# Eight instead of four of the 22 weight steps of each FFN output product computed block-wise with seven products, in a new order

## Chip, cores and metric

One NeuronCore of a Trainium2 chip runs the whole program. The metric is the device time of one execution in microseconds (us), median of several runs. The program has one launch and computes one forward pass of a small two-layer transformer for 256 tokens.

## What is computed

The reference, cut to what matters here. `x` is 256 x 2048, D_MODEL = 2048, D_FF = 5632.

```python
for layer in range(2):
    if layer == 0:   # MLA attention plus attention to 256 memory tokens
        mix = mla_mixer(rms_norm(x, ...), positions, mem, ...)
    else:            # differential attention; keys and values from shared_kv(x)
        k1, k2, v = shared_kv(x, positions, shared_kv_norm, shared_w_kv)
        mix = diff_mixer(rms_norm(x, ...), positions, mem, k1, k2, v, ...)
    x = x + rms_norm(mix, attn_norm_post)
    u = rms_norm(x, ffn_norm_pre[layer]) @ ffn_w_in[layer]        # 2048 -> 11264
    c = conv_b + causal convolution of width 3 of u over the tokens
    h = gelu(c[:, :5632]) * c[:, 5632:]
    x = x + rms_norm(h @ ffn_w_out[layer], ffn_norm_post[layer])  # 5632 -> 2048
```

Everything is float32. The change concerns `h @ ffn_w_out[layer]` in both layers: (256 x 5632) times (5632 x 2048).

## The kernel before

**Arithmetic.** A float32 product is made from three fast ones: every weight block and every activation is split into a high part (the value rounded to the fast format, written by ScalarE) and a low part (value minus high part, written by VectorE); TensorE adds high x high, high x low and low x high into one PSUM bank.

**Steps and rings.** Weights come in steps of 128 partitions x 1024 columns (512 KB: two 128-row chunks of 512 output columns). SyncE (SP) loads a step into `w_raw`, a ring of R = 4 slots; ScalarE (ACT) writes `w_hi`, VectorE (DVE) writes `w_lo`, TensorE (PE) uses both. The semaphores `hi_ready`, `lo_ready` and `step_used` count steps. ACT and DVE are written out by hand in one fixed order: `splits_to(s)` issues all splits up to step s, and epilogues stand between such calls. So a wait inside an epilogue holds back the splits behind it.

**FFN input product (IN0, IN1).** `ffn_in` and `merged_product` (L765 to L806) run 11 iterations of 16 steps per layer: 8 steps for four gate chunks, 8 for four value chunks. In even steps the w_hi products come first, in odd steps the w_lo products. The loops on ACT (L2240 to L2256) and DVE (L3115 to L3140) split weights and, between the splits, form h: `correction` and `corrected` (L3058, L3060), `first_tap`, `other_taps` (L3072), `gate`, `gate_times_value` (L3082), `hi_half`, `lo_half` (L3088). Each loop is in two parts, `(0, PAIRS // 2)` and `(PAIRS // 2, FJ)`. In the first part four more DVE operations on blocks of h (`odd_forms`, `even_forms`), one ACT copy (`sums_hi`, L2236) and one DVE subtraction (`forms_lo`, L3112) make the sums of blocks that the output product needs. The ACT loop stands behind a wait for `x_spilled`: the sums lie where x was, so x has gone to DRAM before.

**Handing over to layer 0's FFN.** After its last operation on the norm (`rstd_row`, L1783), ACT goes into the loop. DVE first waits for that row, adds the late part of the memory values to `vm_b` (L3148, two operations), and goes into its loop.

**FFN output product (OUT0, OUT1).** The output columns are four tiles of 512; each has 22 steps of 2 x 128 rows of the weight. A half is two tiles. For most steps (`plain`, L1277) PE does 2 chunks x 2 token blocks x 3 terms = 12 matmuls of 128x128 by 128x512. For `PAIRS` = 4 of the 22, the same step of both tiles is taken together as a `unit`: as a 2 x 2 block product (two token blocks, two chunks, two tiles) with seven block products instead of eight, 21 matmuls instead of 24. A unit has four entries in the ring, `left` (6 matmuls), `corner` (3), `odd` (6), `even` (6), but two raw slots only. DVE makes the sums of weight blocks (`out_split`, L2392, L2401, L2404); the raws are released by the last of them (`unit_sums`). The order of entries is `out_order`; their slots are `out_slots`. In the first half the order is 9 plain steps of the tile, then units 0 to 3 with 2 plain steps after each, then the rest of that tile, then 18 plain steps of the other tile; the second half is the same. From `UNIT_STARTS` on, for `WIDE` = 40 entries, a fifth slot is used; there the slot's last user is five entries back, at the first unit's `even` entry and elsewhere four.

**Folds and epilogues.** Products shared by several outputs are put together when a half's last unit is done (`fold_copies` on ACT, `fold` on DVE: five operations of 512 columns, L2857 to L2861, and one of 1024, L2865, after the first tile's last step). PE starts the second tile of the half when `folded` says so. `wide_epilogue` then squares the tile on ACT (L2062) and multiplies it by the gain on DVE (L2884). The last tile of a product is `held`: its last HOLD = 4 steps are done for token block 0 first, then for block 1, and its first block needs all four of them. `splits_to(s0 + ends[3])`, which splits the last step, stands behind the third tile's L2884.

**Pool.** GpSimd's queue sends x to DRAM ahead of the FFN (L672), loads the gain row at the start of the output product (L667), and brings x back after the last unit of the second half (L677).

Of the kernel before, what the change touches and what calls it, by code (L numbers as in the profile page):

```python
# [22 lines left out]
P = 128  # L23
# [9 lines left out]
M = 256  # L33
# [24 lines left out]
PAIRS = 4  # L58
# [4 lines left out]

def out_order():
# [13 lines left out]
    ends, unit_ends, unit_starts = [], [], []  # L80
    for half in range(2):
        ks = list(range(PAIRS, FSTEPS))
        for k in ks[:CUT]:
            plain(2 * half, k)
        rest = ks[CUT:]
        unit_starts.append(len(entries))
        for p in range(PAIRS):
            unit(half, p)
            if p == PAIRS - 1:
                unit_ends.append(len(entries))  # L90
            n = 2 if p < PAIRS - 1 else len(rest)
            for k in rest[:n]:
                plain(2 * half, k)
            rest = rest[n:]
        ends.append(len(entries))
        for k in ks:
            plain(2 * half + 1, k)
        ends.append(len(entries))
# [6 lines left out]
WIDE = 40  # L105


def out_slots():
# [11 lines left out]
    assert all(slots[e] == e % R for e in list(range(CUT)) + list(range(OSTEPS - R + 1, OSTEPS)))  # L120
# [124 lines left out]
def program(nc, x_in, mem_in, positions, inv_freq, w, vec, out):  # L245

    with ExitStack() as ctx:
# [19 lines left out]
        raw_flat = w_raw[:, :, :].rearrange("p r n -> p (r n)")  # L267
# [3 lines left out]
        sx_hi = at("sx_hi", [P, PAIRS // 2, 1024], F32R, X0)  # L271
        sx_lo = at("sx_lo", [P, PAIRS // 2, 1024], F32R, X0 + 8 * KB)
# [114 lines left out]
        def unit_quarters(r):  # L387


            a = 1024 * (r % R)  # L390
            assert r % R < R - 1
            return raw_flat[:, a:a + 2048].rearrange("p (q n) -> p q n", q=4)
# [108 lines left out]
        x_back = sem("x_back")  # L501
        ostd_ready = sem("ostd_ready")
# [131 lines left out]
        def _(pool):  # L634
# [56 lines left out]
        def _(pe):  # L691
# [362 lines left out]
            def scores_b(t):  # L1054

                if t in (1, 3, 4, 8, 9):
                    pe.wait_ge(e_ready, T0_B + (t - 1 if t >= 8 else t))
# [211 lines left out]
            def out_product(s0, t0, layer, h_done, turn_done=None):  # L1269
# [22 lines left out]
                def unit(e, kind, p):  # L1292
# [7 lines left out]
                    def s(form, cols, bank):  # L1300
                        o = 256 * form + P * (p % 2)
                        return terms(bank, sx_hi[:, p // 2, o:o + P], sx_lo[:, p // 2, o:o + P],
# [5 lines left out]
                    if kind == "corner":  # L1308
                        return s(3, a, 0)
                    if kind == "odd":  # L1310
                        s(0, a, 1)
                        return s(1, b, 6)
                    s(2, a, 5)
                    return h(1, 1, b, 3)

                for half in range(2):
# [3 lines left out]
                    for e in range(first, OUT_ENDS[2 * half]):  # L1320
                        kind, j, k, _ = OUT_ENTRIES[e]
# [9 lines left out]
                        if half == 0 and k == FSTEPS - 2:  # L1331
                            pe.wait_ge(h_lo, h_done)
                        mm = plain(e, k, 2, range(TT)) if kind == "plain" else unit(e, kind, k)
# [337 lines left out]
        def _(act):  # L1671
# [369 lines left out]
            def fold_copies(s0, half):  # L2041
# [3 lines left out]
                nc.scalar.activation(fold_now[:, 0], ps[:, 1, :], ACT.Copy)  # L2045
# [153 lines left out]
            def ffn_epilogues(layer, s_in, t_in, g_count):  # L2199
# [33 lines left out]
                def sums_hi(i):  # L2233

                    act.wait_ge(s_sums, val(layer * (PAIRS // 2) + 1, 1, i))
                    nc.scalar.activation(sx_hi[:, bass.ds(i, 1), :].rearrange("p a n -> p (a n)"),  # L2236
                                         scratch[:, 0].rearrange("p a b -> p (a b)"), ACT.Copy)\
                        .then_inc(s_hi, 1)

                act.wait_ge(x_spilled, 16 * (layer + 1))  # L2240
                for first, end in ((0, PAIRS // 2), (PAIRS // 2, FJ)):
                    with act.Fori(first, end) as i:
                        for j in range(2):
                            for k in range(DSTEPS):
# [10 lines left out]
                                if ahead == 9 and j == 1 and first == 0:  # L2255
# [102 lines left out]
        def _(dve):  # L2358
# [11 lines left out]
            def out_split(s):  # L2370
# [6 lines left out]
                if kind == "corner":  # L2377
                    nc.vector.tensor_tensor(lo[:, 0:512], unit_quarters(r)[:, 3],
# [8 lines left out]
                if kind == "left":  # L2387

                    quarters, no = unit_quarters(r), raw_no(s0) + r + 1
# [3 lines left out]
                        out_slot(e + 2)[2].rearrange("p (a n) -> p a n", a=2), quarters[:, 0:4:3, :],  # L2393
                        quarters[:, 2].unsqueeze(1).to_broadcast([P, 2, 512]), ALU.add)\
                        .then_inc(odd_sums, 1)
                if kind == "corner":

                    quarters, odd, even = unit_quarters(r), out_slot(e + 1)[2], out_slot(e + 2)[2]
                    dve.wait_ge(step_used, s0 + OUT_USERS[e + 2] + 1)
                    dve.wait_ge(odd_sums, unit_no)  # L2400
                    nc.vector.tensor_tensor(even[:, 0:512], odd[:, 0:512], quarters[:, 3], ALU.add)\  # L2401
                        .then_inc(even_sum, 1)
                    dve.wait_ge(even_sum, unit_no)
                    nc.vector.tensor_tensor(even[:, 512:1024], even[:, 0:512], quarters[:, 1],  # L2404
# [445 lines left out]
            def fold(s0, folds, half):  # L2850
# [199 lines left out]
            def ffn_epilogues(layer, s_in, t_in, g_count):  # L3050
# [28 lines left out]
                def gate_times_value(i):  # L3079
                    dve.wait_ge(pair_dve, val(t_in + 2, 2, i))  # L3080
                    dve.wait_ge(gate_ready, val(g_count + 1, 1, i))
                    nc.vector.tensor_tensor(scratch[:, 1], scratch[:, 0], scratch[:, 1], ALU.mult)\  # L3082
# [224 lines left out]
```

## Time and profile before

| | us |
|---|---|
| median of 3 runs | 2175.74 (2175.74 to 2178.74) |
| the profiled execution | 2175.84 |
| its span | 2174.0 |
| PE busy | 2160.2 (99%) |
| PE weight loads busy | 1870.5 (86%) |
| DVE busy | 1542.9 (71%) |
| ACT busy | 1209.2 (56%) |
| GpSimd busy | 8.9 (0%) |
| DMA | 414.60 MB, mean 191 GB/s |

The 1.84 us between span and time lie outside of what the profile shows. TensorE's granted clock is 9 tenths or more in all of the 40 slices, so no stage is slowed by it. Busy time is the union of an engine's instructions; a matmul's own duration (0.389 us) overlaps with its neighbours', so what a matmul costs is the distance between starts.

### The profile page before, as it was taken

To read this page: it belongs to the slowest core of one execution; us is meant where nothing else is said; L and a number is where in the kernel's file an instruction comes from. 1 tells how busy PE (TensorE), PEld (TensorE's weight loads), DVE (VectorE), ACT (ScalarE), POOL (GpSimd) and SP (SyncE) were. 2 spreads that over 40 slices of the span, in tenths; PEclk is the share of its full clock that TensorE was granted. 3 is DMA by queue.
4 is the path that set the end of the run, shared out by engine and by line. 5 is a ranking of instruction groups with operands and counts; after the bars stand their busy time and mean duration, and the time that the engine had idled before them with its cause. 6 is when DMAs were issued, how large, how long until landed. Compare 5 with 4: busy or idle time off the path is not lost.

```text
span 2174.0 us, 32418 instructions
## 1 busy us (share of the span) xinstructions
PE 2160.2 (99%) x11637; PEld 1870.5 (86%) x11637; DVE 1542.9 (71%) x2172; ACT 1209.2 (56%) x1716; POOL 8.9 (0%) x24
## 2 busy tenths in 40 slices
PE   9999999999999999999999999999999999999998
PEld 8989988888888888888888889888888888888887
DVE  5767756777776767857589877567777776778484
ACT  5745745655555555545465567466555555555353
POOL 0000000000000000000000000000000000000000
PEclk9999999999999999999999999999999999999999
DMA  8565266566566566656756643665655666566665
GB/s 288 176 188 184 82 209 207 175 193 199 178 184 193 186 199 193 213 194 186 249 164 205 196 152 127 202 198 181 204 182 185 191 188 188 183 204 214 200 217 172
DMA packets 202089, 414.60 MB, mean 191 GB/s; under 512 B 12989, under 2 KB 13367, under 8 KB 200719
## 3 DMA queue, kind: packets, MB, share of 16 engines
q1 hardware_dynamic: 200687, 400.29, 58.5%
q0 software_dynamic: 1312, 13.11, 1.7%
q8 instruction: 56, 0.92, 0.2%
q14 instruction: 34, 0.28, 0.0%
HBM read 407.06 MB, written 6.29 MB: 190 GB/s over the span
## 4 chain that ended last, share of the span: by engine, by line
PE 95%; DVE 3%; ACT 1%; issue 1%; DMA 0%; DVEq 0%; ACTq 0%
PE ps L785 27%; PE ps L1277 21%; PE ps L739 20%; PE ps L793 14%; PE ps L823 4%; PE ps L833 3%; PE ps L1518 1%; PE ps L914 1%; DVE scratch L3072 0%; PE ps L1421 0%; PE ps L1044 0%; PE ps L886 0%; PE ps L979 0%; DVE w_lo L2456 0%; ACT w_hi L1738 0%
## 5 line engine op out<-in xcount | busy, mean ns | idle before, releaser
L2456 DVE TENSOR_TENSOR w_lo<-w_raw,w_hi 128x1024 fp32r<-128x1024 f32 x450 | 541.6, 1222 | 261.2 <-ACT w_hi L1738 257.5
L785 PE MATMUL ps<-xT,w_hi 128*128 128x512 f32 x2752 | 657.6, 391 | 0.0
L1738 ACT ACTIVATE w_hi<-w_raw 128x1024 fp32r<-128x1024 f32 (+1 forms) x466 | 475.8, 1042 | 232.6 <-PE ps L739 83.5
L785 PEld LDWEIGHTS ps<-xT,w_hi 128*128 128x128 f32 x2752 | 505.4, 188 | 98.3 <-issue 0.4
L793 PEld LDWEIGHTS ps<-xT,w_lo 128*128 128x128 f32 x2752 | 353.2, 191 | 15.1 <-DVE w_lo L2456 1.6
L793 PE MATMUL ps<-xT,w_lo 128*128 128x256 f32 x2752 | 358.7, 283 | 0.8 <-DVE w_lo L2456 0.8
L2382 DVE TENSOR_TENSOR w_lo<-w_raw,w_hi 128x1024 fp32r<-128x1024 f32 x142 | 171.5, 1223 | 107.4 <-ACT w_hi L1692 106.3
L1277 PE MATMUL ps<-w_hi,hT_hi 128*128 128x512 f32 x624 | 242.8, 389 | 0.0
L1277 PE MATMUL ps<-w_hi,hT_lo 128*128 128x512 f32 x624 | 242.8, 389 | 0.0
L1277 PE MATMUL ps<-w_lo,hT_hi 128*128 128x512 f32 x624 | 242.7, 389 | 0.0
L1692 ACT ACTIVATE w_hi<-w_raw 128x1024 fp32r<-128x1024 f32 x142 | 148.8, 1058 | 133.4 <-PE ps L1277 84.2
L739 PE MATMUL ps<-w_hi,xT 128*128 128x512 f32 x640 | 203.3, 392 | 0.0
L1734 ACT ACTIVATE w_hi<-w_raw,gcol 128x512 fp32r<-128x512 f32 x160 | 106.6, 718 | 62.3 <-PE ps L739 53.0
L739 PEld LDWEIGHTS ps<-w_hi,xT 128*128 128x128 f32 x640 | 120.2, 188 | 24.4
L1277 PEld LDWEIGHTS ps<-w_hi,hT_hi 128*128 128x128 f32 x624 | 117.1, 188 | 24.4
L1277 PEld LDWEIGHTS ps<-w_hi,hT_lo 128*128 128x128 f32 x624 | 117.1, 188 | 24.3
L1277 PEld LDWEIGHTS ps<-w_lo,hT_hi 128*128 128x128 f32 x624 | 117.1, 188 | 24.2
L2443 DVE SCALAR_TENSOR_TENSOR w_lo<-w_raw,gcol,w_hi 128x512 fp32r<-128x512 f32 x160 | 111.9, 748 | 20.3 <-ACT w_hi L1734 19.6
L739 PE MATMUL ps<-w_lo,xT 128*128 128x512 f32 x320 | 124.7, 390 | 0.0
L739 PE MATMUL ps<-w_hi,xbT_hi 128*128 128x512 f32 x256 | 100.1, 391 | 0.0
L739 PE MATMUL ps<-w_hi,xbT_lo 128*128 128x512 f32 x256 | 99.7, 389 | 0.0
L739 PE MATMUL ps<-w_lo,xbT_hi 128*128 128x512 f32 x256 | 99.6, 389 | 0.0
(338 smaller groups left out, 2489.3 us busy)
## 6 DMA issues: line engine op xcount, KB each, us to landing
w_raw<-in_ffn_w_in SPq DMA_DIRECT2D x352, 512.0 KB, 4.1
w_raw<-in_ffn_w_out SPq DMA_DIRECT2D x176, 512.0 KB, 4.8
w_raw<-in_shared_w_kv SPq DMA_DIRECT2D x48, 512.0 KB, 4.3
w_raw<-in_a_w_o SPq DMA_DIRECT2D x32, 512.0 KB, 4.8
w_raw<-in_b_w_in SPq DMA_DIRECT2D x32, 512.0 KB, 4.8
w_raw<-in_b_w_o SPq DMA_DIRECT2D x32, 512.0 KB, 4.5
w_raw<-in_a_w_mem_kv SPq DMA_DIRECT2D x16, 512.0 KB, 6.4
w_raw<-in_b_w_mem_kv SPq DMA_DIRECT2D x16, 512.0 KB, 4.3
```

The costliest lines, as they stand in the source:

```text
L739: mm = nc.tensor.matmul(dst, st, mv, start=first and q == 0, stop=last and q == len(pairs) - 1, skip_group_check=True)
L785: mm = nc.tensor.matmul(ps[:, base + m4, :].rearrange("p (a n) -> p a n", a=2), w_hi[:, slot, cols], xT[:, :, 2 * k + c, :], start=k == c ...
L793: mm = nc.tensor.matmul(ps[:, base + m4, S:2 * S], w_lo[:, slot, cols], xT_hi[:, 2 * k + c, :], start=False, stop=stop and c == 1, skip_gr ...
L823: mm = nc.tensor.matmul(ps[:, bank, 256 * (h % 2):256 * (h % 2) + S], wk[:, P * h:P * (h + 1)], xk, start=bank not in begun, stop=False, s ...
L833: mm = nc.tensor.matmul(ps[:, bank, :], xk[:, tok_t[t]], wk[:, KV_HEADS * P:2 * KV_HEADS * P], start=bank not in begun, stop=False, skip_g ...
L1277: mm = nc.tensor.matmul(ps[:, bank, :], st, mv, start=bank not in begun and q == 0, stop=False, skip_group_check=True)
L1692: a = nc.scalar.activation(hi, w_raw[:, r % R, :], ACT.Copy)
L1734: a = nc.scalar.activation(w_hi[:, s % R, cols], w_raw[:, s % R, cols], ACT.Copy, scale=gcol[:, row:row + 1])
L1738: nc.scalar.activation(w_hi[:, s % R, 0:width], w_raw[:, s % R, 0:width], ACT.Copy)\
L2382: nc.vector.tensor_tensor(lo, w_raw[:, r % R, :], hi.bitcast(F32), ALU.subtract)\
L2443: d = nc.vector.scalar_tensor_tensor(out=w_lo[:, s % R, cols], in0=w_raw[:, s % R, cols], scalar=gcol[:, row:row + 1], in1=w_hi[:, s % R, ...
L2456: nc.vector.tensor_tensor(w_lo[:, s % R, :], w_raw[:, s % R, :], w_hi[:, s % R, :].bitcast(F32), ALU.subtract)\
```

## The change

In the output product eight of the 22 steps become units, instead of four. The shared block product, which was added to bank 1 and copied, now has PSUM bank 7 to itself; of the four sums of h blocks three are left, since that product uses an unsummed block. These three lie in `s32_hi`, `s32_lo` (where x was) and in `s4_hi`, `s4_lo`, where the keys and values of the memory tokens for layer 1 lie. So these go to DRAM and come back (`km_kept`, `vm_kept`, 512 KB each, on GpSimd's queue); ACT waits for both transfers ahead of its loop, next to the wait for x. The plain steps of the second tile go between the units as well; behind the last unit of each half are 3 plain steps of the first tile and 4 of the second. In the first half 9 plain steps lead, in the second 5. The fifth slot is used for 100 entries in one run from the first unit on, and the first unit's `left` takes it.

```diff
-PAIRS = 4
+PAIRS = 8
+LEADS = (CUT, 5)
+REST, TAIL = 3, 4
...
+    ks = range(PAIRS, FSTEPS)
     for half in range(2):
...
+        first, second = ([(2 * half + j, k) for k in ks] for j in range(2))
+        between = first[LEADS[half]:-REST] + second[:-TAIL]
+        for step in first[:LEADS[half]]:
+            plain(*step)
         unit_starts.append(len(entries))
         for p in range(PAIRS):
             unit(half, p)
...
+            gaps = PAIRS - 1
+            for step in between[len(between) * p // gaps:len(between) * (p + 1) // gaps]:
+                plain(*step)
+        unit_ends.append(len(entries))
+        for step in first[-REST:]:
+            plain(*step)
         ends.append(len(entries))
+        for step in second[-TAIL:]:
+            plain(*step)
         ends.append(len(entries))
...
-WIDE = 40
+WIDE = 100
...
-        for e0 in UNIT_STARTS:
-            if e0 <= e < e0 + WIDE:
-                slot = ((e0 + (e - e0) % (R + 1)) % R) if (e - e0) % (R + 1) < R else R
+        turn = e - UNIT_STARTS[0]
+        if 0 <= turn < WIDE:
+            turn = turn % (R + 1)
+            slot = (UNIT_STARTS[0] + turn - 1) % R if turn else R
...
             x_leaves(PIECES_IN0 + len(FFN_PIECES))
+            pool.wait_ge(kv_summed, 1)
+            pool.dma_start(km_kept, kmT_b[:, :, :].rearrange("p h m -> p (h m)"))\
+                .then_inc(kv_spilled, 16)
+            pool.dma_start(vm_kept, vm_b[:, :, :, :].rearrange("p u h n -> p (u h n)"))\
+                .then_inc(kv_spilled, 16)
             gain_rows_of("ffn_post0", gain_f, OUT0)
             x_returns(OUT0)
+            pool.dma_start(kmT_b[:, :, :].rearrange("p h m -> p (h m)"), km_kept)\
+                .then_inc(kv_back, 16)
+            pool.dma_start(vm_b[:, :, :, :].rearrange("p u h n -> p (u h n)"), vm_kept)\
+                .then_inc(kv_back, 16)
...
                     if kind == "corner":
-                        return s(3, a, 0)
+                        return s(s4_hi, s4_lo, 0, a, 0)
                     if kind == "odd":
-                        s(0, a, 1)
-                        return s(1, b, 6)
-                    s(2, a, 5)
+                        t1, t3 = odd_columns(r)
+                        h(0, 1, t1, 7)
+                        return s(s32_hi, s32_lo, 0, t3, 6)
+                    s(s32_hi, s32_lo, 256, a, 5)
                     return h(1, 1, b, 3)
...
                 act.wait_ge(step_used, s0 + UNIT_ENDS[half])
-                nc.scalar.activation(fold_now[:, 0], ps[:, 1, :], ACT.Copy)
                 nc.scalar.activation(fold_kept[:, 0], ps[:, 4, :], ACT.Copy).then_inc(fold_copied, 1)
...
+                act.wait_ge(kv_spilled, 32)
                 act.wait_ge(x_spilled, 16 * (layer + 1))
                 for first, end in ((0, PAIRS // 2), (PAIRS // 2, FJ)):
...
-                                if ahead == 9 and j == 1 and first == 0:
+                                if ahead == 8 and j == 1 and first == 0:
                                     sums_hi(i)
...
-                p1, u3, q5, u2 = (fold_kept[:, 0], fold_kept[:, 1], fold_now[:, 0], fold_now[:, 1])
-                nc.vector.tensor_tensor(ps[:, 0, :], ps[:, 0, :], q5, ALU.add)
+                p1, u3, u2 = fold_kept[:, 0], fold_kept[:, 1], fold_now[:, 0]
                 link(nc.vector.tensor_tensor(u2, ps[:, 5, :], p1, ALU.add))
-                nc.vector.tensor_tensor(ps[:, 0, :], ps[:, 0, :], u2, ALU.subtract)
                 link(nc.vector.tensor_tensor(u3, ps[:, 6, :], u2, ALU.add))
-                nc.vector.tensor_tensor(ps[:, 1, :], ps[:, 1, :], u3, ALU.subtract)\
+                nc.vector.tensor_tensor(fold_now[:, 0], ps[:, 7, :], u2, ALU.subtract)
+                link(nc.vector.tensor_tensor(fold_now[:, 1], ps[:, 7, :], u3, ALU.subtract))
+                nc.vector.tensor_tensor(ps[:, 0:2, :], ps[:, 0:2, :], fold_now, ALU.add)\
                     .then_inc(folded, 1)
...
-                nc.vector.tensor_tensor(vm, late_sum[:, u, :], vm, ALU.add)
+                d = nc.vector.tensor_tensor(vm, late_sum[:, u, :], vm, ALU.add)
+            d.then_inc(kv_summed, 1)
```

On DVE's loop the two sums of `odd_forms` stand in `gate_times_value` now, one made in place, ahead of `h_ready`; `even_forms` stands ahead of `lo_half`; `forms_lo` is two subtractions of 512 and 256 columns. The loop parts become iterations 0 to 3 and 4 to 10.

## Rows read from the trace of the kernel before

**Rows 1.** The page: busy times of the engines, share of the span, instructions.

```profile
PE 2160.2 (99%) x11637; PEld 1870.5 (86%) x11637; DVE 1542.9 (71%) x2172; ACT 1209.2 (56%) x1716; POOL 8.9 (0%) x24
```

**Rows 2.** Waits of PE, whole span: line, releaser, us, times, longest.

```profile
PE ps L1277 <- DVE w_lo L2385: 2.4, 4, 0.6
```

**Rows 3.** Timeline of PE at unit 0, layer 0: start, us, what, idle before.

```profile
871.65 0.39 PE L1277 MATMUL ps<-w_hi,hT_lo 128*128 128x512 f32 x1
...
881.85 0.39 PE L1277 MATMUL ps<-w_hi,sx_lo 128*128 128x512 f32 x1
...
882.85 0.50 PE L1277 MATMUL ps<-w_hi,sx_hi 128*128 128x512 f32 x1 [0.61 <-DVE w_lo L2385]
```

**Rows 4.** Timeline of DVE, units 0 and 1, layer 0.

```profile
880.24 0.69 DVE L2401 TENSOR_TENSOR w_sum<-w_sum,w_raw 128x512 f32<-128x512 f32 x1 [0.82 <-PE ps L1277]
880.97 0.69 DVE L2404 TENSOR_TENSOR w_sum<-w_sum,w_raw 128x512 f32<-128x512 f32 x1
881.58 2.44 DVE L2385 TENSOR_TENSOR w_lo<-w_sum,w_hi 128x1024 fp32r<-128x1024 f32 x2
...
887.20 1.23 DVE L2382 TENSOR_TENSOR w_lo<-w_raw,w_hi 128x1024 fp32r<-128x1024 f32 x1 [0.92 <-ACT w_hi L1692]
...
890.79 0.69 DVE L2404 TENSOR_TENSOR w_sum<-w_sum,w_raw 128x512 f32<-128x512 f32 x1
```

**Rows 5.** Timeline of ACT: the first split of unit 1, held by its load.

```profile
886.10 1.06 ACT L1692 ACTIVATE w_hi<-w_raw 128x1024 fp32r<-128x1024 f32 x1 [1.45 <-DMA w_raw<-in_ffn_w_out]
```

**Rows 6.** Timelines, layer 0: DVE (unit 3, both folds), then ACT (second fold).

```profile
910.21 0.69 DVE L2404 TENSOR_TENSOR w_sum<-w_sum,w_raw 128x512 f32<-128x512 f32 x1
...
918.75 0.69 DVE L2857 TENSOR_TENSOR ps<-ps,y_f 128x512 f32<-128x512 f32 x1
...
1042.53 1.23 DVE L2865 TENSOR_TENSOR ps<-ps,y_f 128x1024 f32<-128x1024 f32 x1 [0.18 <-PE ps L1277]
...
1045.37 1.22 DVE L2884 TENSOR_TENSOR y_f<-ps,gain_f 128x1024 f32<-128x1024 f32 x1
...
1043.80 0.60 ACT L2062 ACTIVATE scratch<-ps 128x512 bf16<-128x512 f32 x1 [4.50 <-DVE ps L2865]
```

**Rows 7.** Timelines of ACT, then DVE, start of layer 0's FFN loop.

```profile
384.84 1.28 ACT L1738 ACT_TABLE_LOAD   x1
386.13 2.01 ACT L1738 ACTIVATE w_hi<-w_raw 128x1024 fp32r<-128x1024 f32 x2
...
384.91 1.29 DVE L3148 TENSOR_TENSOR vm_b<-late_sum,vm_b 128x512 f32<-128x512 f32 x2 [1.64 <-ACT rstd_row L1783]
...
399.82 4.62 DVE L2456 TENSOR_TENSOR w_lo<-w_raw,w_hi 128x1024 fp32r<-128x1024 f32 x4
```

**Rows 8.** Timeline of PE, same stretch, and one iteration later.

```profile
388.83 2.08 PE L793 MATMUL ps<-xT,w_lo 128*128 128x256 f32 x16
...
399.97 2.35 PE L793 MATMUL ps<-xT,w_lo 128*128 128x256 f32 x16
...
441.12 3.82 PE L785 MATMUL ps<-xT,w_hi 128*128 128x512 f32 x16
...
447.34 3.81 PE L785 MATMUL ps<-xT,w_hi 128*128 128x512 f32 x16
```

**Rows 9.** The DMA view, whole span: count, KB each, median us to landing.

```profile
x<-x_kept POOLq DMA_DIRECT2D x2, 2048.0 KB, 10.4
...
gain_o<-in_a_attn_norm_post POOLq DMA_DIRECT2D x1, 1024.0 KB, 9.1
gain_ob<-in_b_attn_norm_post POOLq DMA_DIRECT2D x1, 1024.0 KB, 4.6
...
out<-x SPq DMA_DIRECT2D x1, 512.0 KB, 2.7
```

**Rows 10.** Timelines of DVE and POOL: x to DRAM, layer 0.

```profile
363.03 1.94 DVE L2906 SCALAR_TENSOR_TENSOR x<-y_o,nrm,x 128x512 f32<-128x512 f32 x2
...
365.26 0.56 POOL L672 DMA_DIRECT2D x_kept<-x  x1 [83.09 <-DVE x L2906]
```

More of the change, by code:

```diff
@@ L119, in out_slots @@
         last[slot] = e
-    assert all(slots[e] == e % R for e in list(range(CUT)) + list(range(OSTEPS - R + 1, OSTEPS)))
+    assert all(slots[e] == e % R for e in list(range(CUT)) + list(range(OSTEPS - R, OSTEPS)))
     assert EXTRA % R == 0 and OSTEPS % R == 0
@@ L385, in out_slot, with unit_blocks, odd_columns @@
             return w_hi[:, slot], w_lo[:, slot], w_sum[:, slot]
[L387 to L392, printed above, removed]
+        def unit_blocks(r):
+            left, right = 2 * (r % R), 2 * ((r + 1) % R)
+            outer = slice(left, left + 4, 3) if left < right else slice(right + 1, left + 1, 5)
+            return (raw_blocks[:, outer, :], raw_blocks[:, left + 1], raw_blocks[:, right],
+                    raw_blocks[:, right + 1])
+        def odd_columns(r):
+            low, high = slice(0, 512), slice(512, 1024)
+            return (low, high) if r % R < R - 1 else (high, low)
         def mem_gain_row(s):
@@ L501, in program @@
         x_back = sem("x_back")
+        kv_summed = sem("kv_summed")
+        kv_spilled = sem("kv_spilled")
+        kv_back = sem("kv_back")
         ostd_ready = sem("ostd_ready")
@@ L1054, in scores_b @@
             def scores_b(t):
+                if t == BH:
+                    pe.wait_ge(kv_back, 32)
                 if t in (1, 3, 4, 8, 9):
@@ L1290, in plain, with unit @@
                     return mm
-                def unit(e, kind, p):
+                def unit(e, kind, p, r):
                     wh, wl, _ = out_slot(e)
@@ L1330, in out_product @@
                         pe.wait_ge(lo_ready, s0 + e + 1)
-                        if half == 0 and k == FSTEPS - 2:
+                        if half == 0 and (j, k) == (0, FSTEPS - 2):
                             pe.wait_ge(h_lo, h_done)
-                        mm = plain(e, k, 2, range(TT)) if kind == "plain" else unit(e, kind, k)
+                        mm = plain(e, k, 2 - 2 * (j % 2), range(TT)) if kind == "plain" else \
+                            unit(e, kind, k, r)
                         mm.then_inc(step_used, 1)
@@ L3110, in forms_lo @@
                     dve.wait_ge(s_hi, val(layer * (PAIRS // 2) + 1, 1, i))
+                    flat = scratch[:, 0].rearrange("p a b -> p (a b)")
                     at_i = lambda b: b[:, bass.ds(i, 1), :].rearrange("p a n -> p (a n)")
-                    nc.vector.tensor_tensor(at_i(sx_lo), scratch[:, 0].rearrange("p a b -> p (a b)"),
-                                            at_i(sx_hi).bitcast(F32), ALU.subtract).then_inc(s_lo, 1)
-                for first, end, links in ((0, PAIRS // 2, 6), (PAIRS // 2, FJ, 4)):
+                    nc.vector.tensor_tensor(at_i(s32_lo), flat[:, 0:512], at_i(s32_hi).bitcast(F32),
+                                            ALU.subtract)
+                    nc.vector.tensor_tensor(at_i(s4_lo), flat[:, 512:768], at_i(s4_hi).bitcast(F32),
+                                            ALU.subtract).then_inc(s_lo, 1)
+                for first, end, links in ((0, PAIRS // 2, 7), (PAIRS // 2, FJ, 4)):
                     linked[0] = before - links * first
```

93 lines of the change are left out of this document (44 added, 49 removed).

## The prediction

> **What bounds the kernel now.** I read the engines' busy times first: PE is busy 99% of the span, DVE 71%, ACT 56% [rows 1]. So only two things move the end: matmuls, and gaps between matmuls. The view of PE's waits says that the gaps are few: in the output products PE waited for a low part four times, at the first unit of each half [rows 2]. The timeline there gives both prices. Between 871.65 and 881.85 lie 45 starts of matmuls: 0.2267 us each. Then the `odd` entry starts 1.00 us after the last matmul of `corner`: a gap of 0.77 us beyond the pitch [rows 3]. Then I read the timelines of DVE and ACT for how early they are where PE does not wait, since the change gives them more to do per matmul, and moves two epilogues.
>
> **Matmuls removed.** A unit has 21 matmuls instead of 24. 8 more units per layer (4 in each half), two layers: 16 x 3 = 48. 48 x 0.2267 = **-10.9 us**, all on the path.
>
> **The first unit's gap.** At unit 0 the sum for `even` waited for PE's last plain step: DVE began it at 880.24 after 0.82 us of waiting, finished the second sum at 881.66, and the low part of `odd` followed [rows 4]; PE wanted `odd` at 882.08 and got it at 882.85 [rows 3]. The slot's last user was four entries back. With the new slots it is five back (and the first unit's `left` takes the extra slot), so the sum is released 2.72 us earlier, more than the gap. 4 x 0.77 = **-3.1 us**. But 100 wide entries from entry 9 end at entry 108, and by the new order the last unit of the second half is entries 109 to 112. It is back on four slots, behind plain steps, as unit 0 was: 0.77 in each layer, **+1.5 us** (0 to 1.5).
>
> **Units in a row.** What a turn from one unit to the next costs is read from the sums: done at 881.66 and 891.48, so 9.82 us [rows 4]. That is the ring of raws: the load of the next unit lands 4.44 us after the sums (886.10) [rows 5], then high part, low part, sums. DVE's own work in it is 6.5 us for the unit (887.20 to the second sum's end at 891.4, and two low parts [rows 4]) and 1.155 for a plain step (4.62 for four [rows 7]). PE's turn is 21 x 0.2267 = 4.76 plus 2.72 per plain step: 10.20 with two. Gaps in the new order: 1, 2, 2, 1, 2, 2, 2 plain steps in the first half, 2, 2, 2, 3, 2, 2, 3 in the second. With one, the right raw alone waits for the sums: DVE's work decides, 6.5 + 1.155 = 7.7 against PE's 7.48. With three: load, then three sums, some 11.3 against 12.9. So a half's turns take 2 x 7.7 + 5 x 9.82 = 64.5 against PE's 66.0, and 71.7 against 76.8. Lead at the first `odd` is 0.9 us by the new slots (sums done at 879.9, low part at 881.1, wanted at 882.1), 0.6 after the first turn. I take **0**. The cover is thin: 0.4 us per turn of two.
>
> **FFN input loops.** Four iterations instead of two make sums of h. The work per iteration stays (four operations of 256 columns and one of 1024 become four and two of 768 in all). But ACT's copy comes one step earlier, ahead of the last high part instead of behind it. In the second iteration of the kernel before, PE's groups start 6.22 us apart (441.12 to 447.34) where 5.57 is the pitch (388.83 to 399.97 is two): 0.65 lost, since that copy and a table load delay the loop's first split [rows 8]. Moved, it starts some 1.5 us earlier. **-1.3 us** for two layers (0 to -1.3). The other iterations keep a lead of half a microsecond at the tightest low part: 0.
>
> **The end of a second half.** This is where the new order costs. Behind the last unit PE has 3 plain steps, then the last tile's 4, held, where the first block's fourth step is wanted after 3 x 6 matmuls. Time from the sums of the last unit, U. PE: `odd` starts at U+1.2 [rows 3, 4], the unit ends at U+4.0, the last tile starts at U+12.2 and wants its fourth step at U+16.3. DVE: the fold starts at U+7.85 (910.90 to 918.75), since four splits with freshly released raws stand ahead of it [rows 6]; four operations of 512 columns and one of 1024 are 4.0: U+11.9, just in time for the last tile; two splits, 2.3: U+14.2; then the fold's end, ACT's squares, the multiplication by the gain, 1042.53 to 1046.59 or 4.06 [rows 6]: U+18.3; only then the last split: U+19.5. PE stands 3.2 us in each layer, **+6.4 us**. If the fold is done early the chain hangs on the last tile's start alone: 12.2 + 4.06 + 1.2 - 16.3 = 1.2 each, 2.4; 0.5 more for slower loads, 7.4. Before, 18 steps covered this. In the first half nothing waits (the fourth step, not held, is wanted 4 us later). x starts back at U+4.4 and lands 10.4 later [rows 9], before DVE wants it.
>
> **The new wait ahead of ACT's loop.** In layer 0 ACT now waits until keys and values are in DRAM. They are complete when DVE's two additions end, 384.91 + 1.29 = 386.20, and these themselves wait for ACT's last operation before the loop [rows 7]. So the wait can't be over when ACT comes to it at 384.84. POOL starts 0.3 us after its release (364.97 to 365.26), an issue takes 0.56 [rows 10]: the second transfer is issued at 387.05. 512 KB from SP's queue to DRAM landed in 2.7, 1024 KB on POOL's in 4.6 and in 9.1 [rows 9]. I take 4.0 for the second transfer, nearest to 4.6 for both together, since ACT's standstill also stops the weight loads: 391.1. Behind the waiting ACT stand its table load and the high parts of steps 9 and on; all start 391.1 - 384.84 = 6.3 us later. PE has 1.4 us in hand at step 9, but none at step 13: its low part ended at 401.0, where PE's group is 0.27 us longer than the others [rows 7, 8], and the chain from step 9 to there (split, correction, taps, split) has no slack. So **+6.3 us** (4.9 by 2.7 us, 10.8 by 9.1). In layer 1 the wait is long over.
>
> By the Trainium skill, "DMA: Bandwidth & Descriptors", section "Anatomy of one DMA — SWDGE (gpsimd) path", such a transfer takes about 2.0 us plus its bytes at 436 GB/s, most of the 2.0 for the receipt of the write, DRAM being the slowest target. It would give 4.4 us for both, and the term 5.9 instead of 6.3. For 2 MB it gives 6.8, where the trace has 10.4 beside the weight loads.
>
> **Sum.** -10.9 - 3.1 + 1.5 - 1.3 + 6.4 + 6.3 = -1.1. On the profiled execution's 2175.84 (0.1 above the median of the runs, so nothing to correct): **2174.7 us**. Low ends: -10.9 - 3.1 + 0 - 1.3 + 2.4 + 4.9 = -8.0, 2167.8. High ends: -10.9 - 3.1 + 1.5 + 0 + 7.4 + 10.8 = +5.7, 2181.5.
>
> **Rivals.**
> (a) ACT's new wait is covered. For it: one small transfer, and ACT is busy 56% only. Against: the additions start after ACT's own last work. It would give 2174.7 - 6.3 = 2168.4. Chance 0.1.
> (b) The end of the second half costs nothing, because the last split runs ahead of the epilogue. Against: the order on DVE is written out. 2174.7 - 6.4 = 2168.3. Chance 0.1. Both, 2162.0: 0.05.
> (c) Slower: the ring of raws decides. A turn of two plain steps has 0.4 us of cover, with a landing 4.44 us after the sums. If loads land later than 4.8, each such turn loses the difference. At 5.4 it is 0.6 for each of 20 turns, less some 4 us that the leads of four halves absorb: +8, 2182.7. For it: the input product's start and x's return show loads crowding each other. Against: bytes per matmul hardly change. Chance 0.15.
> (d) The change does not do what it says (fewer matmuls are not removed): PE's count would not be 11637 - 48. 0.01.
>
> **Chances.** The forecast has 0.59, and within it 2170 to 2180. A difference within 0.2%, 4.35 us, is about what a measurement can't tell from none. Faster by more: (a), (b), both, and a little of the forecast's low ends, 0.28. Slower by more: (c) and the forecast's high ends, 0.19. Same: 0.53. The range reaches over (a) and (b), and to the high ends: 2167.5 to 2181.5; out of it are both rivals at once and most of (c).
>
> **What would show it.** PE with 11589 matmuls. A wait of ACT's L1738 of some 6 us at 385 to 391 for a transfer, and PE idle in two pieces, some 5 at step 9 and 1.4 at step 13. No PE wait at the first units; one of 0.6 at entry 111. A PE wait of some 3 us for the last split, 8 us before the end of each output product. Second iteration of the input loops without its 0.6. I would be wrong if PE waits at many units (c), or if one of the two large waits is absent.

## The result and the profile after

The changed kernel takes 2188.66 us (median, 2187.0 to 2191.18); the kernel before took 2177.24 alongside. The ratio is 1.0056, interval 1.0044 to 1.0068: slower by 11 us, where 1 less was forecast and 2181.5 was the upper end. The profiled execution took 2188.01, its span is 2185.8, 11.8 above before.

The page of the kernel after, busy times, answers to [rows 1]:

```profile
PE 2157.1 (99%) x11589; PEld 1866.7 (85%) x11589; DVE 1624.2 (74%) x2280; ACT 1249.0 (57%) x1764; POOL 11.0 (1%) x28
```

The 48 matmuls are gone (11637 to 11589), yet PE's busy time fell by 3.1 us only, not by 10.9: matmuls became longer somewhere. PE's waits, kernel after, whole span (line, releaser, us in total, times, longest), answer to [rows 2]:

```profile
PE ps L1308 <- DVE w_lo L2416: 11.8, 4, 4.0
PE ps L822 <- DVE w_lo L2492: 4.8, 1, 4.8
PE ps L1308 <- DVE w_lo L2419: 1.2, 2, 0.6
```

L1308 is the output product (L1277 before), L822 the input product's low part (L793 before), L2416 and L2492 the splits. The third line is the forecast gap at entry 111, twice; the waits at the first units are gone. The first two are the costs that I had put at 3.2 us in each layer and at 6.3 us.

To divide the 11.8 us among stages, take the start of the first matmul of each stage from PE's timelines. Before: `rstd` transposed at 384.02, output product of layer 0 at 855.54, next stage at 1092.19, output product of layer 1 at 1930.88, its last matmul at 2166.39. For the kernel after the same rows are:

```profile
383.66 0.38 PE L963 MATMUL ps<-ident,rstd 128*128 128x128 f32 x2
...
861.80 0.39 PE L1308 MATMUL ps<-w_hi,hT_hi 128*128 128x512 f32 x1
...
1101.92 0.40 PE L1551 MATMUL ps<-w_hi,xbT_hi 128*128 128x512 f32 x1
...
1939.94 0.39 PE L1308 MATMUL ps<-w_hi,hT_hi 128*128 128x512 f32 x1
...
2178.22 0.39 PE L1308 MATMUL ps<-w_hi,hT_lo 128*128 128x512 f32 x1
```

| stage | before | after | difference | forecast |
|---|---|---|---|---|
| up to `rstd` | 384.02 | 383.66 | -0.4 | 0 |
| input product, layer 0 | 471.52 | 478.14 | +6.6 | +5.6 |
| output product, layer 0 | 236.65 | 240.12 | +3.5 | -3.0 |
| up to the output product, layer 1 | 838.69 | 838.02 | -0.7 | -0.6 |
| output product, layer 1 | 235.51 | 238.28 | +2.8 | -3.0 |

The forecast of an output product is half of -10.9 - 3.1 + 1.5 + 6.4. Two of the five stages are off by 6 us each, and in both the cause is at the end of the second half (the input product of layer 0 is off by 1). Its timeline on PE, layer 0, kernel after (start, us, what, idle before):

```profile
1082.79 0.39 PE L1308 MATMUL ps<-w_hi,hT_lo 128*128 128x512 f32 x1
1087.16 0.79 PE L1308 MATMUL ps<-w_hi,hT_hi 128*128 128x512 f32 x1 [3.98 <-DVE w_lo L2416]
1087.75 0.63 PE L1308 MATMUL ps<-w_lo,hT_hi 128*128 128x512 f32 x1
1088.18 0.63 PE L1308 MATMUL ps<-w_hi,hT_lo 128*128 128x512 f32 x1
...
1092.26 0.80 PE L1308 MATMUL ps<-w_hi,hT_hi 128*128 128x512 f32 x1 [2.17 <-DVE w_lo L2416]
...
1096.23 0.39 PE L1308 MATMUL ps<-w_hi,hT_hi 128*128 128x512 f32 x1
...
1099.43 0.39 PE L1308 MATMUL ps<-w_hi,hT_lo 128*128 128x512 f32 x1
```

From 1082.79 to 1099.43 there are 30 starts after the first. At 0.2267 us [rows 3] they would take 6.80; they took 16.64. That is 9.84 lost: 3.98 + 2.17 = 6.15 standing (PE idle), and 3.7 more, nearly all of it in matmuls that start 0.43 us apart (1087.75, 1088.18) instead of 0.227. (0.3 of the 3.7 is that each stand costs 0.16 more between starts than it has idle time, as 0.77 against 0.61 in [rows 3].) ACT and then GpSimd at the same place show why PE stood:

```profile
1075.98 1.06 ACT L1725 ACTIVATE w_hi<-w_raw 128x1024 fp32r<-128x1024 f32 x1 [0.67 <-DMA w_raw<-in_ffn_w_out]
1084.79 1.06 ACT L1725 ACTIVATE w_hi<-w_raw 128x1024 fp32r<-128x1024 f32 x1 [7.74 <-DMA w_raw<-in_ffn_w_out]
...
1072.60 0.53 POOL L697 DMA_DIRECT2D x<-x_kept  x1 [209.81 <-PE ps L1308]
1073.12 0.53 POOL L707 DMA_DIRECT2D kmT_b<-km_kept  x1
1073.64 0.53 POOL L709 DMA_DIRECT2D vm_b<-vm_kept  x1
```

ACT waited 7.74 us for the raw of the last tile's third step. DMA view of the same kernel, 1070 to 1090 (target and source, queue, count, KB each, median us from issue to landing):

```profile
x<-x_kept POOLq DMA_DIRECT2D x1, 2048.0 KB, 10.5
w_raw<-in_ffn_w_out SPq DMA_DIRECT2D x3, 512.0 KB, 12.0
```

A weight load took 12.0 us beside x's return (with keys and values behind it in layer 0); 4.44 is what I had reckoned for a landing behind the sums. Layer 1 has the same loss where x alone comes back; the same view, kernel after, 2148 to 2168:

```profile
x<-x_kept POOLq DMA_DIRECT2D x1, 2048.0 KB, 11.2
w_raw<-in_ffn_w_out SPq DMA_DIRECT2D x3, 512.0 KB, 11.2
```

So keys and values add little to it. Of the three loads of layer 0, the one issued 1 us ahead of x landed in 4.4 us, and the two issued behind x in 12.0 and 12.7, later than x itself.

The low part of the fourth step stands behind the epilogue on DVE as foretold (kernel after):

```profile
1085.88 1.23 DVE L2416 TENSOR_TENSOR w_lo<-w_raw,w_hi 128x1024 fp32r<-128x1024 f32 x1 [4.75 <-ACT w_hi L1725]
1087.02 1.23 DVE L2901 TENSOR_TENSOR ps<-ps,y_f 128x1024 f32<-128x1024 f32 x1
1089.85 1.22 DVE L2920 TENSOR_TENSOR y_f<-ps,gain_f 128x1024 f32<-128x1024 f32 x1
1090.99 1.22 DVE L2416 TENSOR_TENSOR w_lo<-w_raw,w_hi 128x1024 fp32r<-128x1024 f32 x1
```

So first the load is late, then the whole epilogue (L2901, squares on ACT, L2920) follows, and then the last split: the second wait of 2.17.

The granted clock is in the view by windows (stretch, its length, busy us and counts of PE, weight loads, DVE, ACT, GpSimd, then the clock, DMA share, GB/s), kernel after:

```profile
1080.00:1086.00 6.00, 3.18 (x15) 2.29 (x13) 1.25 (x3) 1.06 (x1) 0.00 (x0) 0.99 0.99 393
1086.00:1092.00 6.00, 2.93 (x6) 1.82 (x6) 4.63 (x6) 2.21 (x5) 0.00 (x0) 0.50 0.77 273
1092.00:1098.00 6.00, 5.74 (x17) 4.64 (x18) 2.12 (x4) 1.80 (x5) 0.00 (x0) 0.65 0.28 87
```

After PE had stood for 3.98 us the clock was 0.50, the 1.2 GHz level, and it was back at 2.4 GHz by the matmul at 1096.23. That is why the starts lie 0.43 apart and not 0.227.

The start of layer 0's loop, kernel after, ACT and then PE, answers to [rows 7, 8]:

```profile
390.71 1.28 ACT L1771 ACT_TABLE_LOAD   x1 [6.24 <-DMA vm_kept<-vm_b]
392.00 2.00 ACT L1771 ACTIVATE w_hi<-w_raw 128x1024 fp32r<-128x1024 f32 x2
...
394.37 2.08 PE L822 MATMUL ps<-xT,w_lo 128*128 128x256 f32 x8 [4.78 <-DVE w_lo L2492]
396.24 5.50 PE L814 MATMUL ps<-xT,w_hi 128*128 128x512 f32 x16
```

ACT waits 6.24 us for the keys and values; 391.1 was forecast for the end of the wait, 390.71 came. PE's group of 16 takes 5.50 instead of 3.82 at full clock: again slow matmuls behind a stand of 4.78. The stage lost 6.6 + 0.65 (the gain of its second iteration) = 7.3.

### The profile page after: what moved, and what is told of

It reads as the page before. It is cut to its first block, busy times and chain, and to the rows that moved or that the text cites. A ratio compares the mean times of both kernels' runs of the same rounds, so it can differ in the third digit from the quotient of the medians.

```text
span 2185.8 us, 32593 instructions
## 1 busy us (share of the span) xinstructions
PE 2157.1 (99%) x11589; PEld 1866.7 (85%) x11589; DVE 1624.2 (74%) x2280; ACT 1249.0 (57%) x1764; POOL 11.0 (1%) x28
## 4 chain that ended last, share of the span: by engine, by line
PE 96%; DVE 2%; DMA 1%; ACT 1%; issue 0%; DVEq 0%; POOL 0%; SPq 0%; ACTq 0%
PE ps L814 29%; PE ps L768 20%; PE ps L1308 20%; PE ps L822 15%; PE ps L852 4%; PE ps L862 3%; DMA w_raw<-in_ffn_w_out 1%; PE ps L1551 1%; PE ps L943 1%; PE ps L1454 0%; PE ps L1073 0%; DVE w_lo L2416 0%; PE ps L915 0%; PE ps L1008 0%; PE ps L1079 0%; PE ps L1104 0%
## 5 line engine op out<-in xcount | busy, mean ns | idle before, releaser
L2492 DVE TENSOR_TENSOR w_lo<-w_raw,w_hi 128x1024 fp32r<-128x1024 f32 x450 | 541.4, 1221 | 263.2 <-ACT w_hi L1771 259.1
L822 PEld LDWEIGHTS ps<-xT,w_lo 128*128 128x128 f32 x2752 | 353.9, 192 | 18.6 <-DVE w_lo L2492 5.2
L822 PE MATMUL ps<-xT,w_lo 128*128 128x256 f32 x2752 | 359.0, 283 | 4.8 <-DVE w_lo L2492 4.8
L1308 PE MATMUL ps<-w_hi,hT_hi 128*128 128x512 f32 x576 | 227.4, 395 | 13.0 <-DVE w_lo L2416 11.8
L1308 PE MATMUL ps<-w_lo,hT_hi 128*128 128x512 f32 x576 | 226.5, 393 | 0.0
L1308 PE MATMUL ps<-w_hi,hT_lo 128*128 128x512 f32 x576 | 226.2, 393 | 0.0
L2416 DVE TENSOR_TENSOR w_lo<-w_raw,w_hi 128x1024 fp32r<-128x1024 f32 x126 | 152.5, 1223 | 23.4 <-ACT w_hi L1725 16.3
L1725 ACT ACTIVATE w_hi<-w_raw 128x1024 fp32r<-128x1024 f32 x126 | 132.5, 1060 | 50.9 <-DMA w_raw<-in_ffn_w_out 34.2
L1308 PEld LDWEIGHTS ps<-w_hi,hT_hi 128*128 128x128 f32 x576 | 109.4, 190 | 38.9 <-DVE w_lo L2416 14.0
L1308 PEld LDWEIGHTS ps<-w_hi,hT_lo 128*128 128x128 f32 x576 | 109.6, 190 | 23.0
L1308 PEld LDWEIGHTS ps<-w_lo,hT_hi 128*128 128x128 f32 x576 | 109.6, 190 | 22.5
L2479 DVE SCALAR_TENSOR_TENSOR w_lo<-w_raw,gcol,w_hi 128x512 fp32r<-128x512 f32 x160 | 111.9, 748 | 20.6 <-ACT w_hi L1767 20.0
L1727 ACT ACTIVATE w_hi<-w_sum 128x1024 fp32r<-128x1024 f32 x64 | 68.0, 1062 | 103.0 <-DVE w_sum L2427 55.9
```

Source lines behind the costliest of these rows:

```text
L822: mm = nc.tensor.matmul(ps[:, base + m4, S:2 * S], w_lo[:, slot, cols], xT_hi[:, 2 * k + c, :], start=False, stop=stop and c == 1, skip_gr ...
L1308: mm = nc.tensor.matmul(ps[:, bank, :], st, mv, start=bank not in begun and q == 0, stop=False, skip_group_check=True)
L1725: a = nc.scalar.activation(hi, w_raw[:, r % R, :], ACT.Copy)
L1727: a = nc.scalar.activation(hi, sums_now, ACT.Copy)
L2416: nc.vector.tensor_tensor(lo, w_raw[:, r % R, :], hi.bitcast(F32), ALU.subtract)\
L2479: d = nc.vector.scalar_tensor_tensor(out=w_lo[:, s % R, cols], in0=w_raw[:, s % R, cols], scalar=gcol[:, row:row + 1], in1=w_hi[:, s % R, ...
```

## The experiments

Two suspects for 19 us (the two ends) and one for 7 (the start) had to be parted, and the other terms tested by what is left without them. "Less than after" compares medians that were taken at different times. Alongside them the kernel before had 2177.24 (four runs, 2175.74 to 2180.32), 2176.22 and 2175.96, so such a difference is sure to about 1 us only; the stages of the profiled executions part the costs more finely.

**The wait ahead of ACT's loop, moved.** Nothing is left out; ACT waits just before it first writes over the keys.

```diff
+                    act.wait_ge(kv_spilled, 32)
                     act.wait_ge(s_sums, val(layer * (PAIRS // 2) + 1, 1, i))
...
-                act.wait_ge(kv_spilled, 32)
                 act.wait_ge(x_spilled, 16 * (layer + 1))
```

> The changed kernel, with ACT's wait for keys and values in DRAM moved from ahead of the loop to ahead of the first copy that overwrites them. Theory: that wait alone held ACT 6.2 us in layer 0, PE lost 7.3 us there (6.2, and 1.1 by a granted clock that fell to half after 4.8 us of standing): 7.3 us less than the changed kernel's 2188.7, 2181.4, and granted clock 1.0 between 385 and 405. Rival: the two transfers crowd the weight loads of the loop's start; they are still there, so the time stays within 2 us and PE still waits for w_lo there.

Measured: 2180.62, ratio to before 1.0021 (1.0012 to 1.0031); 8.0 less than after. Both transfers are still there. ACT's timeline and the windows of this kernel:

```profile
384.85 1.28 ACT L1771 ACT_TABLE_LOAD   x1
...
395.00:400.00 5.00, 5.00 (x30) 4.35 (x29) 4.55 (x10) 3.50 (x5) 0.00 (x0) 1.00 0.59 193
```

The table load begins right behind ACT's last operation on the norm, at 384.85 as before, PE is busy for all of the window and the clock stays at 1.00. From `rstd` (384.03) to the output product (854.90) it is 470.87, 7.3 less than after. So the term is the wait alone, not the traffic: rival (a) is false for the kernel as changed, and its price was right within the clock. In this profile both ends cost some 1.1 us more than in that of after (output products 241.27 and 239.37), so its span is only 4.6 less: the size of the ends, too, moves by about a microsecond from one execution to another.

**Nothing comes back.** x, keys and values are set to zero on GpSimd instead of being loaded again, so the output isn't the model's from there on; all other work stays.

```diff
-                pool.dma_start(x[:, :, :].rearrange("p t n -> p (t n)"), x_kept).then_inc(x_back, 16)
+                nc.gpsimd.memset(x[:, :, :], 0.0).then_inc(x_back, 16)
...
-            pool.dma_start(kmT_b[:, :, :].rearrange("p h m -> p (h m)"), km_kept)\
-                .then_inc(kv_back, 16)
+            nc.gpsimd.memset(kmT_b[:, :, :], 0.0).then_inc(kv_back, 16)
...
```

> The changed kernel, but x, keys and values are not brought back from DRAM: GpSimd sets them to zero in place (that part of the computation is left out). Theory crowding: at the end of each output product the loads of the last steps land 12 us after issue because x's return of 2 MB is on the queues; without it the third of the four last steps isn't late, and what remains is the last split behind the epilogue, 3.1 us in each layer, at full clock: 2 x (8.8 - 3.1) = 11.4 less than 2188.7, 2177.3. Rival order: the place of the last split makes the loss; then PE's 4 us wait stays and the time falls by under 2 us.

Measured: 2177.67, 1.0005 (0.9995 to 1.0014), 11.0 less than after. How long `w_raw` took to land between 1070 and 1090, first in the kernel after, then in this one:

```profile
DMA to landing us min/median/max: 4.2/10.5/12.7
```

```profile
DMA to landing us min/median/max: 3.7/4.9/5.7
```

PE at the same place, this kernel, and the view by windows:

```profile
1090.30 0.50 PE L1306 MATMUL ps<-w_hi,hT_hi 128*128 128x512 f32 x1 [2.77 <-DVE w_lo L2414]
```

```profile
1090.00:1095.00 5.00, 4.70 (x20) 3.86 (x21) 2.38 (x5) 2.51 (x6) 0.00 (x0) 1.00 0.33 105
```

One wait of 2.77 is left in each layer, for the last split behind the epilogue, and in the window 1090 to 1095 the granted clock is 1.00. That is the chain of my forecast at its price: 3.2 foretold, and 3.2 lost, since the output product of layer 0 takes 233.37 here, 229.37 where nothing waits (with ten steps behind the last unit, below), and 0.77 is entry 111; 3.3 in layer 1 by the same count (232.3 against 228.25). What came back made the rest: 9.8 - 3.2 = 6.6 in layer 0 and 9.3 - 3.3 = 6.0 in layer 1, 12.6 in all (the 9.3 is 238.28 less the same 228.25 and 0.77). The whole kernel gained less, 11.0: its profiled execution stood longer at the start of the loop (6.4 instead of 4.8), and about 1.5 us of the time went there.

Nothing was changed at that start, so its cost is not a fixed one. In the six profiles that keep the wait ahead of the loop (after, this one, the next two, x in four, ten steps) PE stood 4.8 to 6.6 us there, and the input product of layer 0 took 477.1 to 480.3 us, 6.2 to 9.4 more than the 470.87 without the wait.

**The last split ahead of the epilogue.** Nothing is left out. ACT and DVE do the last tile's fourth split before the third tile's epilogue.

```diff
-                    splits_to(s0 + ends[j] + AHEAD)
+                    splits_to(s0 + ends[j] + AHEAD + (folds is not None and j == 2))
...
+                act.wait_ge(pair_act, t0 + 3)
                 last_tile(0).then_inc(bank_squared, 1)
...
-                splits_to(s0 + OUT_ENDS[2 * half] + AHEAD)
+                splits_to(s0 + OUT_ENDS[2 * half] + AHEAD + half)
```

> The changed kernel, with the second half's last weight split ahead of the third tile's epilogue on ACT and DVE. Theory crowding plus order: PE's wait of 4.0 for the third of the last four steps stays, its wait of 2.2 for the fourth goes, with some of the half clock behind it: 2.5 to 4 us in each layer, 5 to 8 less than 2188.7, 2181 to 2184. Rival order alone: both waits go, 17 us less, 2171. Rival crowding alone: nothing changes, 2188.

Measured: 2182.44, 1.0024 (1.0014 to 1.0034), 6.2 less than after. Each end has one wait now, but of 4.0 and 3.6, not none; waits of PE in this kernel:

```profile
PE ps L1308 <- DVE w_lo L2417: 7.6, 2, 4.0
```

The load is as late as ever; ACT in this kernel:

```profile
1087.35 1.06 ACT L1725 ACTIVATE w_hi<-w_raw 128x1024 fp32r<-128x1024 f32 x1 [8.08 <-DMA w_raw<-in_ffn_w_out]
```

By the stages the output products take 237.44 and 235.80 us, 2.7 and 2.5 less than after: the order on DVE is the smaller part of the loss also while the other cause is there.

**Both of them.** Zeros again for x, keys and values; edits as above.

> Both of the last two edits together (x, keys and values set to zero instead of brought back: left out). Theory crowding plus order: PE doesn't wait at the end of either output product, and the clock stays at full: 2 x 8.8 = 17.6 less than 2188.7, 2171.1. Any rival by which seven products or the fold itself cost the time there leaves more than 2 us of waits.

Measured: 2169.51, 0.9969 (0.9958 to 0.998), 19.2 less than after. No wait of PE is left at either end, and the stages tell the same: 230.30 for the output product of layer 0 and 229.16 for that of layer 1, 9.8 and 9.1 less than after. So these two causes with their slow clock are all of the ends' 19.1 (9.8 and 9.3), within 0.2 us. 11.0 and 6.2 add up to 17.2, not 19.2. In the profiles the gain of the first was lessened by the longer start of its loop, and in the second the stand of 4.0 kept its slow matmuls.

**x in four pieces.** Nothing is left out: 512 KB of x come back after every second unit of the second half, keys and values in the next stage.

```diff
-                pool.wait_ge(step_used, s_out + UNIT_ENDS[1])
-                pool.dma_start(x[:, :, :].rearrange("p t n -> p (t n)"), x_kept).then_inc(x_back, 16)
+                for a in range(PAIRS // 2):
+                    e = OUT_ENTRIES.index(("even", 2, 2 * a + 1, OUT_ENTRIES[UNIT_AT[2 * a + 1]][3]))
+                    pool.wait_ge(step_used, s_out + e + 1)
+                    pool.dma_start(x[:, :, 512 * a:512 * (a + 1)],
+                                   x_kept.rearrange("p (t n) -> p t n", t=TT)[:, :, 512 * a:512 * (a + 1)])\
+                        .then_inc(x_back, 16)
...
```

> The changed kernel, with x brought back in four pieces of 512 KB, each once the two units that read the sums lying in its place are done, and with keys and values brought back later, in the next product. Theory crowding: what held the last loads was 2 MB and 1 MB issued at once after the last unit; with a quarter of that the loads land in time, and only the last split behind the epilogue is left, 2.9 us of standing in each layer as in the run without the return: 2177 to 2179. Rival: any transfer issued at that place holds the loads; then PE's wait of 4 us stays, 2187.

Measured: 2180.85, 1.0017 (1.0008 to 1.0027), 7.8 less than after and 2 us above what was expected. The loads land within 6.9 us between 1060 and 1095 (12.7 at the most in the kernel after), and what is left is the order on DVE, now dearer. Waits of PE in this kernel, then the one of layer 0 and the view by windows behind it:

```profile
PE ps L1314 <- DVE w_lo L2422: 6.0, 2, 3.3
```

```profile
1087.92 0.50 PE L1314 MATMUL ps<-w_hi,hT_hi 128*128 128x512 f32 x1 [2.77 <-DVE w_lo L2422]
```

```profile
1089.00:1093.00 4.00, 4.00 (x12) 3.15 (x11) 2.14 (x3) 1.63 (x5) 0.00 (x0) 0.57 0.40 131
```

The 3.3 is in layer 1, where 2.8 was left without any return: there ACT waits 3.67 us for the load of the third step, issued just behind the last quarter of x, and the epilogue stands behind that step's split. In layer 0 the stand is 2.77, as without the return, but the clock was low behind it (0.57 in 1089 to 1093), and the output product took 234.97, 1.6 more than the 233.37 without the return.

**Ten steps behind the last unit instead of four.** Nothing is left out; six plain steps of the last tile move from between the units of the second half to behind them. It gives the late load and the epilogue 6 x 2.72 = 16.3 us of cover, and at the same time leaves one plain step between some units.

```diff
-REST, TAIL = 3, 4
+REST, TAILS = 3, (4, 10)
...
-        between = first[LEADS[half]:-REST] + second[:-TAIL]
+        between = first[LEADS[half]:-REST] + second[:-TAILS[half]]
```

> The changed kernel with one number changed: behind the last unit of each second half stand 10 plain steps of the last tile instead of 4, so fewer between the units (1, 1, 2, 1, 2, 1, 2). Theory of the prediction, cover: x's return, the epilogue and the last split are all covered by the longer tail, and the last unit is on five slots; 2 x 8.8 and 2 x 0.77 us less than 2188.7: 2169.6, with no PE wait in the output products. The single steps between units should cost nothing (DVE 7.7 against PE 7.5 a turn). Rival (c) of the prediction: the ring of raws or DVE bounds turns with one plain step; then PE waits at units, 0.2 to 0.6 each, and the gain is 2 to 5 us less.

Measured: 2167.85, 0.9958 (0.9942 to 0.9973), 20.8 less than after. PE waits nowhere in the output products; both take 229.4 and 228.3 us. The gap at entry 111 is gone as well, since the last unit now lies within the 100 wide entries: 19.1 + 1.5 = 20.6. Rival (c) would have shown here first, at turns with one plain step: there is no wait, so the ring of raws keeps up with units that stand closer together than the change has them.

**Ten steps, and the wait moved.** Nothing is left out. This is the kernel after without both causes.

> The last kernel, and ACT's wait for keys and values moved into the loop as in the run with the late wait. Both edits add, since they are in different stages: 8.0 us less than the run with ten steps, 2161.6, or 0.993 of the kernel before; that is the matmuls removed (10.9), the first units' gaps (3.1) and the input loops' (1.3). Rival: the units cost something that the stalls hid; then it stays above 2165.

Measured: 2160.18 (2160.07 to 2163.81), 0.9928 (0.9914 to 0.9941): 28.5 less than after and faster than both kernels. The page of this kernel:

```profile
PE 2148.2 (100%) x11589; PEld 1862.4 (86%) x11589; DVE 1620.5 (75%) x2280; ACT 1248.7 (58%) x1764; POOL 11.0 (1%) x28
```

It is the test of the whole sum: with the two costs gone and entry 111 covered, the rest of my terms must stand alone. -10.9 - 3.1 - 1.3 = -15.3; on 2175.96, the kernel before alongside, 2160.7. Its span is 2158.5 against 2174.0: -15.5. The crowding is not gone. GpSimd and DVE of this kernel, end of layer 0's output product:

```profile
1048.73 0.53 POOL L697 DMA_DIRECT2D x<-x_kept  x1 [192.59 <-PE ps L1308]
...
1062.80 1.23 DVE L2416 TENSOR_TENSOR w_lo<-w_raw,w_hi 128x1024 fp32r<-128x1024 f32 x1 [1.81 <-ACT w_hi L1725]
```

DVE's split is still held up 14 us after x starts back, by a high part whose load is late; the six steps only keep PE busy meanwhile, as the 18 did before the change.

**Every cost by its own remedy.** x in four, keys and values later, the wait moved, the last split first and the fifth slot for 105 entries instead of 100.

```diff
-WIDE = 100
+WIDE = 105
```

> The changed kernel in its own order of steps, with: x in four pieces, keys and values back later, ACT's wait in the loop, the last split ahead of the epilogue, and five slots up to the last unit. Each part's own theory adds up: 17.6 + 8.0 + 1.5 less than 2188.7: 2161.6, the same as the long tail. Rival: the last piece of x still crowds the last loads; 1 to 4 us more.

Measured: 2163.38, 0.9937 (0.9924 to 0.9951): 1.8 above the expectation and 3.2 more than the ten steps give. Waits of PE in this kernel:

```profile
PE ps L1314 <- DVE ps L2904: 1.9, 2, 0.9
```

That is no split but the fold itself: after three plain steps its results are 0.9 us late for the last tile. It is the link of my chain that the forecast called "just in time". Loads on time and the last split first are not enough to make it show: with both, and 100 wide entries, PE did not wait there, but it lost its 0.77 at entry 111 shortly before. With 105 entries PE comes that much earlier, while the four splits ahead of the fold wait for slots that PE frees. ACT in this kernel, at the last of them:

```profile
1068.49 1.06 ACT L1731 ACTIVATE w_hi<-w_raw 128x1024 fp32r<-128x1024 f32 x1 [1.37 <-PE ps L1314]
```

How the 0.9 divides between the two was not run apart. The output products take 230.61 and 229.50, 1.2 us above those with ten steps. The expectation's rival, the last piece of x, is not what is seen: no wait of PE for a split is left.

## Why the prediction was wrong

- **Matmuls, -10.9.** Right: 11589, and the sum closes only with it (last run but one).
- **First unit, -3.1; last unit, +1.5.** Right: no wait at the first units, 0.6 twice at L2419, gone where ten steps or 105 entries cover it.
- **Units in a row, 0.** Right, with more cover than I saw: turns of one plain step in the second half cost nothing either. Rival (c) is excluded.
- **Input loops, -1.3.** Right. PE's rows one iteration later, kernel after, where [rows 8] had 6.22 us between groups: 448.03 - 442.46 = 5.57.

```profile
442.46 3.82 PE L814 MATMUL ps<-xT,w_hi 128*128 128x512 f32 x16
446.11 2.08 PE L822 MATMUL ps<-xT,w_lo 128*128 128x256 f32 x16
448.03 2.23 PE L814 MATMUL ps<-xT,w_hi 128*128 128x512 f32 x9
```

- **The wait ahead of ACT's loop, +6.3.** Right as a stand: ACT came 6.2 us later than before (390.71 against 384.84 - 0.36 for the earlier `rstd`). The stage lost 7.3, because I reckoned all of PE's matmuls at full clock; 1.1 is the longer distance of their starts behind the stand. Other profiles with the same wait lost 6.2 to 9.4 there, so the 7.3 is one draw of several. I also split it in two stands of PE (5 and 1.4); it was one of 4.8 and slow matmuls. By the Trainium skill, "DMA: Bandwidth & Descriptors", section "Anatomy of one DMA — SWDGE (gpsimd) path", the two transfers would take 4.4 us; from the first one's issue at 386.14 to ACT's next instruction at 390.71 it was 4.6, so the trace agrees. (By the forecast's own count the 4.4 would have made the term 6.1, from 386.49 + 4.4 - 384.84, and not the 5.9 that it gives.)
- **The end of a second half, +6.4.** This is the step that failed: the mechanism was there and the size was not. 3.2 an end was forecast, 9.8 and 9.3 came, 19.1 in all. The chain that I wrote (fold, epilogue, last split) costs 3.2, as the run without the return shows. What I left out is that x's return, for which I only asked whether x itself lands in time, slows the last weight loads to 12 us. The kernel before had shown it: its loads between 1034 and 1046, beside x's return (issued at 1034.63), were as follows.

```profile
DMA to landing us min/median/max: 7.1/8.7/10.2
```

  I had read past them since PE did not wait there; 18 plain steps lay behind. Rival (c) even named x's return as a place where loads crowd each other, but priced it at the units and not at the last four steps. My upper bound, "0.5 more for slower loads", was the wrong one: these rows were nearer to the case than 4.44, with 8.7 - 4.4 to 10.2 - 4.4, some 4 to 6 us more. In front of a tile that wants its third step 12 matmuls after its start, there is nothing to hide that. On top of it comes the clock, most of the 3.7 in layer 0. I had no row for it: the longest wait of PE in the whole kernel before is 1.0.
- **The sum.** With the measured terms: -10.9 - 3.1 + 1.5 - 1.3 + 7.3 + 19.1 = +12.6; the stages have +12.2 from `rstd` on, and the span +11.8 with the 0.4 by which `rstd` came earlier.

Of the late loads, x's 2 MB is by far the larger part and the 1 MB of keys and values behind it a small one: layer 1, where only x comes back, has loads of 11.2 us against 12.0 and lost 9.3 against 9.8. The two were not run apart within layer 0. What stays open is why a load waits so long beside that transfer, and why the stand at the loop's start differs from profile to profile.

## What to carry to other kernels

When a change shortens the stretch of work behind a large transfer, price each load that is in flight beside that transfer by the landing times which the trace shows there, even if nobody waited for them: they were hidden by the stretch that is being removed. Ask of a wait that is added which is the first instruction that needs it, and put it there: here that was worth some 7 us for one moved line (7.3 by the stage, 8.0 by the medians). Before a stand of PE of several microseconds is summed, add the slow matmuls behind it.

## What the hardware showed beyond that

A stand of PE of a few microseconds can cost more than its own time, because the granted clock is at the 1.2 GHz level during its end or behind it. Behind 3.98 us it was 0.50, and around the 4.78 us at the loop's start it was low as well (windows of the kernel after):

```profile
390.00:396.00 6.00, 1.63 (x7) 1.63 (x8) 2.91 (x3) 5.14 (x5) 0.00 (x0) 0.75 0.06 14
396.00:402.00 6.00, 6.00 (x23) 4.90 (x22) 3.79 (x4) 3.91 (x6) 0.00 (x0) 0.68 0.73 245
```

In the second window PE is busy throughout, and yet its group of 16 took 5.50 us where 3.82 is the time at full clock.

The length of the stand alone does not tell whether this happens. In all ten profiles every stand of 3.2 us or more had the low clock with it, and none of 1.6 us or less brought it. But 2.77 us came out both ways: without the return the clock stayed at 1.00 behind it, and with x in four pieces, layer 0, it was 0.57 over 1089 to 1093, and the output product took 1.6 us longer. So a stand of about three microseconds needs two prices, one at full clock and one with slow matmuls behind it. What else decides, these runs don't tell.
